# Gate building shared with GpSimd: every fourth group's one-hot rows made token by token, VectorE's keys and gates read from PSUM

## The chip, the cores and the metric

The kernel runs on one core of a Trainium2 chip, in one launch, in float32 (a few index steps in bfloat16 and integers). The metric is device time in microseconds, the median of several runs; one further execution was taken with the hardware profiler.

## The reference

A trunk of two layers over 512 tokens of width 1024. Each layer is a mixer (a Conformer convolution in layer 0, stick-breaking attention in layer 1) and a PEER layer of single-neuron experts; each part is pre-normalised and modulated by adaLN vectors. The change is in the PEER layers:

```
q = (h @ w_q)                                  # 8 heads, 2 halves of 128
s = einsum(q, sub_keys)                        # 128 scores per head and half
top_s, top_i = top_k(s, 16)                    # per half
best_s, best_c = top_k(all sums of the two halves, 16)
experts = i1 * 128 + i2                        # 128 picks a token
gates = softmax(best_s)
act = gelu(u_tab[experts] . h) * gates
y = sum over picks of act * v_tab[experts]
```

## The kernel before, in words

The two tables of a layer have 16384 rows of 1024 floats each. The tokens are split in two halves of 256. The first half is computed densely: TensorE multiplies all 128 blocks of 128 experts (`u_block`, L922, 512 KB of `u_t` each; `v_block`, L931, 512 KB of `pk_v` each), and VectorE multiplies the gelu of a block by a matrix of gates that is zero for experts not picked (L1663). The second half is computed by gathering: for each of 128 picks, in two quarters of 128 tokens, GpSimd asks for one row of either table per token by an indirect DMA (`u_row`, L492; `v_row`, L498; 512 KB each), VectorE makes the dot product (`u_dot`, L1584) and adds the weighted row (`v_add`, L1601). Rows of u land in eight slots, rows of v in four; a request waits until its slot has been used, and requests of u and v alternate on GpSimd's one queue.

The gate matrix is made by TensorE: for each token, a [picks x 128] one-hot of the second key times a [picks x 64] one-hot of the first key weighed by the gate. "First gates" is the stage in which this is done for keys 0 to 63 of the first key, ahead of the dense blocks of round g=0; those for keys 64 to 127 are made between the dense blocks of g=0 (`hots`, `gates_group`). Round g=1 has dense blocks and gathering alone.

First gates has 32 groups of 8 tokens. `picks_t_full` says that keys and gates are turned (picks on partitions) in PSUM (L885), ScalarE copies them to SBUF as `pick_t` (L1244, L1245), and then for each group:

- VectorE, `first_hots`: the first key's one-hots (L1630, 8 tokens x 64), the second key's (L1632, 8 x 128), and gates times the first four tokens' one-hots (L1636). Both buffers (`hot1`, `hot2`) have two slots, so group n may start when TensorE is done with group n-2.
- ScalarE, `weigh_hots`: gates times the other four tokens' one-hots (four operations, L1267).
- TensorE, `first_gates`: 8 matmuls (16 in the profile, two for each) into one of two pairs of PSUM banks (L903). For the even group both banks are called mid, for the odd group they are acc and out_e.
- ScalarE, `take_gates`: two copies of 128x256 to the gate matrix (L1252), which free the pair of banks.

VectorE runs the groups in 8 chunks of four, and behind each chunk one `u_dot` of the first batch of gathered rows (behind the first chunk the softmax of the second half as well, L1577 to L1579). Order on each engine is program order. Ahead of first gates VectorE ranks the last heads (`rank`), GpSimd looks up what they picked (`look_up`, L531 to L543), and VectorE's marking for the next look-up (`choose`, L1491) waits for the look-up two heads back or one. GpSimd's look-up of the last head ends inside first gates; after it come the first eight u rows, then `both`. TensorE clears the banks of the dense sums with 1-row matmuls (`clear`, L889: out_e 0 to 2 before `u_block(0, 0)`, out_e 3 after first gates), and the first `u_block` runs ahead of first gates.

## Time and profile before

| what | value |
|---|---|
| median of 3 runs | 3123.57 us (3122.34 to 3128.29) |
| the profiled execution, own time | 3127.49 us |
| its span, first to last instruction | 3125.7 us |
| TensorE matmul / weight load busy | 2901.2 us (93%) / 2087.0 us (67%) |
| VectorE busy | 2306.6 us (74%) |
| ScalarE busy | 534.6 us (17%) |
| GpSimd busy | 1509.3 us (48%) |
| DMA, mean over the span | 306 GB/s |

The order of time lists an operation's start, its duration, engine, line and tiles; records of one line that follow one another stand in one row with their count, and brackets hold the idle time of the engine before it and what ended that. The stretches view gives, for a window, the busy time and count of records by engine, then the granted TensorE clock as a share of full speed, the busy share of the DMA engines and what they moved. Groups by form give total busy time and the mean duration in ns, then the idle time before. GpSimd is POOL, VectorE DVE, ScalarE ACT, TensorE PE. Positions in us count from the span's start.

### The profile page before, as it was taken

Reading aid. Unit: us, or ns where it says so; the run is one execution under the profiler, and the core shown is the slowest. Engines: PE = TensorE matmul, PEld = TensorE weight load, DVE = VectorE, ACT = ScalarE, POOL = GpSimd, SP = SyncE. Lnnn points to the kernel's source line nnn. Section 1 sums busy time; section 2 is a strip of 40 time slices with the busy share of each in tenths; the row PEclk is TensorE's granted clock in tenths of the full one; section 3 lists DMA queues with packets and bytes.
Section 4 is the critical chain, followed back from the end, with each engine's and each line's share of the span. In section 5 each row is a group of like instructions: output and inputs, shape, how many; then the busy total and the mean of one; then the engine's idle time right before and its main releaser. Section 6 shows DMA issues by size and latency. Waiting matters only on the chain. (4 is left out here: it accounts for less than half of the span.)

```text
span 3125.7 us, 45269 instructions
## 1 busy us (share of the span) xinstructions
PE 2901.2 (93%) x12846; PEld 2087.0 (67%) x12846; DVE 2306.6 (74%) x4886; ACT 534.6 (17%) x1358; POOL 1509.3 (48%) x1567
## 2 busy tenths in 40 slices
PE   6998988999999999999899988969999999999997
PEld 4786777777777665555587866767776676655554
DVE  3999799888878766676522654998788888667666
ACT  2122216100000000000232243152000000000001
POOL 0001354455655676676300252454555555777774
PEclk8998989999999999999999999989999999999999
DMA  7644454799999999999733322336999999999998
GB/s 300 241 175 162 162 210 127 291 409 393 409 410 404 409 410 410 410 410 410 267 140 109 134 81 81 108 121 237 410 406 401 403 405 410 410 410 410 410 410 319
DMA packets 242632, 956.16 MB, mean 306 GB/s; under 512 B 26938, under 2 KB 27114, under 8 KB 224875
## 3 DMA queue, kind: packets, MB, share of 16 engines
q0 software_dynamic: 147456, 536.94, 43.6%
q1 hardware_dynamic: 95082, 418.12, 34.7%
q8 instruction: 41, 0.67, 0.1%
q14 instruction: 53, 0.43, 0.0%
HBM read 952.85 MB, written 2.10 MB: 306 GB/s over the span
## 5 line engine op out<-in xcount | busy, mean ns | idle before, releaser
L931 PE MATMUL out_e<-weights,mod_rows 128*128 128x512 f32 x2048 | 933.4, 599 | 61.6 <-DVE mod_rows L1663 58.6
L922 PE MATMUL acc<-h_t,weights 128*128 128x256 f32 x4096 | 930.7, 380 | 0.0
L922 PEld LDWEIGHTS acc<-h_t,weights 128*128 128x128 f32 x4096 | 781.0, 191 | 218.3 <-issue 121.5
L498 POOL DMA_INDIRECT v_rows<-in_pk_v,idx_now x512 | 634.7, 1240 | 563.7 <-DVE mod_rows L1601 440.1
L1601 DVE SCALAR_TENSOR_TENSOR mod_rows<-v_rows,dots_acts,mod_rows 128x1024 f32<-128x1024 f32 x512 | 657.8, 1285 | 221.8 <-DMA v_rows<-in_pk_v,idx_now 207.7
L931 PEld LDWEIGHTS out_e<-weights,mod_rows 128*128 128x128 f32 x2048 | 376.0, 190 | 471.2 <-issue 371.3
L492 POOL DMA_INDIRECT u_rows<-in_pk_u,idx_now x512 | 576.4, 1126 | 235.7 <-issue 152.1
L1584 DVE SCALAR_TENSOR_TENSOR u_rows<-u_rows,h_rows 128x1024 f32<-128x1024 f32 x512 | 625.8, 1222 | 82.5 <-DMA u_rows<-in_pk_u,idx_now 78.5
L531 POOL CAST top_f<-top_i 128x64 f32<-128x64 uint32 x32 | 7.6, 236 | 717.0 <-DVEq L1542 709.0
L1287 ACT ACTIVATE mod_rows<-acc 128x256 f32<-128x256 f32 x256 | 96.9, 383 | 1168.2 <-PE acc L922 816.9
L612 PE MATMUL acc<-h_t,weights 128*128 128x256 f32 x1024 | 237.4, 393 | 12.5 <-ACT h_t L1085 8.4
L612 PE MATMUL acc<-u_rows,weights 128*128 128x256 f32 x1024 | 228.7, 383 | 5.9 <-ACT u_rows L1085 5.0
L612 PEld LDWEIGHTS acc<-h_t,weights 128*128 128x128 f32 x1024 | 200.7, 198 | 45.7 <-ACT h_t L1085 9.2
L1663 DVE TENSOR_TENSOR mod_rows<-mod_rows,region 128x256 f32<-128x256 f32 x256 | 109.7, 429 | 161.7 <-ACT mod_rows L1287 108.1
L612 PEld LDWEIGHTS acc<-u_rows,weights 128*128 128x128 f32 x1024 | 195.1, 192 | 33.8 <-ACT u_rows L1085 5.6
L1425 DVE SCALAR_TENSOR_TENSOR region<-region,cols 128x256 f32<-128x256 f32 x480 | 191.1, 478 | 0.1
L912 PEld LDWEIGHTS mid<-scratch 128*128 128x128 f32 x1024 | 124.2, 192 | 4.4 <-DVE scratch L1622 1.2
L912 PE MATMUL mid<-scratch 128*128 128x64 f32 x1024 | 121.4, 272 | 0.4 <-DVE scratch L1622 0.4
L604 PE MATMUL acc<-weights,region 128*128 128x256 f32 x512 | 116.9, 386 | 0.5 <-ACT region L1154 0.5
L604 PEld LDWEIGHTS acc<-weights,region 128*128 128x128 f32 x512 | 96.9, 192 | 18.9 <-issue 5.3
L903 PE MATMUL mid<-scratch 128*128 128x128 f32 x512 | 67.3, 286 | 41.0 <-DVE scratch L1636 41.0
L1240 ACT ACTIVATE dots_acts<-dots_acts (+1 forms) x64 | 13.4, 209 | 523.6 <-DVEq L1589 443.3
(246 smaller groups left out, 2362.9 us busy)
## 6 DMA issues: line engine op xcount, KB each, us to landing
weights<-in_u_t SPq DMA_DIRECT2D x256, 512.0 KB
weights<-in_pk_v SPq DMA_DIRECT2D x256, 512.0 KB
weights<-in_pk SPq DMA_DIRECT2D x32, 1024.0 KB, 4.8
v_rows<-in_ada SPq DMA_DIRECT2D x30, 1024.0 KB, 7.2
weights<-in_w_qkv SPq DMA_DIRECT2D x24, 1024.0 KB, 4.8
weights<-in_w_in SPq DMA_DIRECT2D x16, 1024.0 KB, 7.8
weights<-in_ada SPq DMA_DIRECT2D x8, 1024.0 KB, 4.8
weights<-in_w_out SPq DMA_DIRECT2D x8, 1024.0 KB, 4.8
```

The source lines that it names most:

```text
L492: nc.gpsimd.indirect_dma_start(u_rows[:, r, :], None, a["pk_u"], bass.IndirectOffsetOnAxis(ap=idx_now[:, 0, par, r:r + 1], axis=0)).then_i ...
L498: nc.gpsimd.indirect_dma_start(v_rows[:, r % VR, :], None, a["pk_v"], bass.IndirectOffsetOnAxis(ap=idx_now[:, 1, par, r:r + 1], axis=0)).t ...
L604: last = nc.tensor.matmul(to[:, tt * NC:(tt + 1) * NC], lhs(k, tt), w[:, k * NC:(k + 1) * NC], start=k == 0 and bias is None, stop=k == KB ...
L612: last = nc.tensor.matmul(to[:, c * HALF:(c + 1) * HALF], w[:, k * NC + c * P:k * NC + (c + 1) * P], columns_of[h][:, k, :], start=k == 0, ...
L912: last = nc.tensor.matmul(mid[s][:, t * ROUND:(t + 1) * ROUND], hot2[:, s, t, :], hot1[:, s, t, :], start=True, stop=True)
L922: last = nc.tensor.matmul(acc[s][:, 0:HALF], weights[:, s, k * P:(k + 1) * P], h_t[:, k, :], start=k == 0, stop=k == KB - 1)
L931: last = nc.tensor.matmul(out_e[2 * tt + c][:, :], e_act[:, s, tt * P:(tt + 1) * P], weights[:, s, D + c * 512:D + (c + 1) * 512], start=F ...
L1287: nc.scalar.activation(e_act[:, n % 2, :], acc[n % 2][:, 0:HALF], ACT.Gelu).then_inc(e_gelu_ready, 1)
L1425: steps.behind(stt_op(out=to, in0=seen, scalar=tap, in1=to, op0=ALU.mult, op1=ALU.add))
L1584: stt_op(out=u_rows[:, r, :], in0=u_rows[:, r, :], scalar=1.0, in1=h_rows[:, q % 2, :], op0=ALU.mult, op1=ALU.mult, accum_out=dots[:, bass ...
L1601: stt_op(out=y[:, :], in0=v_rows[:, r % VR, :], scalar=acts[:, bass.ds(b * BATCH + r, 1)], in1=y[:, :], op0=ALU.mult, op1=ALU.add).then_in ...
L1663: tt_op(e_now, e_now, gate, ALU.mult).then_inc(e_act_ready, 1)
```

## The change

The groups keep their order on TensorE, but every fourth (n = 3, 7, ..., 31, eight a layer) is made by GpSimd in buffers of its own, one slot each (`pool_hot1` in `region`, `pool_hot2` in `mod_rows`): for each of the 8 tokens one `tensor_scalar` of 128 elements with one per-partition scalar and one of 64 elements with two (`fourth_hots`, 16 operations a group; it weighs all eight tokens, so ScalarE has nothing to weigh there). VectorE makes the other 24 groups, three in each chunk, numbered m on their own; its slots alternate in m. VectorE reads keys and gates in PSUM, where TensorE now turns them (out_e 0 and 1), in place of `pick_t`; ScalarE still copies `pick_t`, for GpSimd, for its own scales and for g=0. Because out_e 0 and 1 hold the keys, they are cleared after first gates. GpSimd asks for the first two u rows of the first batch between the last look-ups, for the other six and the first half of the next batch between its groups. The loops over groups on TensorE, ScalarE and VectorE are written out, and so are the first two batches of `both`.

```diff
--- before.py
+++ after.py
@@ -139,11 +139,11 @@
...
     @contextmanager
-    def loop(self, times, per):
+    def loop(self, times, per, start=0):
...
         base, static = self.count, self.static
-        with self.engine.Fori(0, times) as i:
-            self.count = i * per + base
+        with self.engine.Fori(start, start + times) as i:
+            self.count = i * per + (base - start * per)
             yield i
...
@@ -227,6 +227,9 @@
...
+        pool_hot2 = mod_rows[:, 2 * D:3 * D].rearrange("p (t n) -> p t n", t=GROUP)
+        pool_hot1 = region[:, 0:GROUP * ROUND].rearrange("p (t n) -> p t n", t=GROUP)
+
...
@@ -280,6 +283,7 @@
...
         first_turned = [out_e[2:4], acc]
+        turned_picks = [out_e[0][:, 0:HALF], out_e[0][:, HALF:2 * HALF], out_e[1][:, 0:HALF]]
         mean, var = out_e[1][:, 0:HALF], out_e[2][:, 0:HALF]
...
@@ -356,6 +361,21 @@
...
         block = ctx.enter_context(nc.Block())
+
+        FOURTH = 4
+        ITERS = GROUPS // FOURTH
+        OWN = GROUPS - ITERS
+
+        def own_no(n):
+
+            return n // FOURTH * (FOURTH - 1) + n % FOURTH
+
+        def group_of(m):
+
+            return m // (FOURTH - 1) * FOURTH + m % (FOURTH - 1)
+
+        def by_pool(n):
+            return n % FOURTH == FOURTH - 1
...
@@ -504,14 +524,31 @@
...
-            def both(q, b, par, after):
+            def both(q, b, par, after, between={}, behind_u=None):
                 indices(q, b, par, 1)
...
                         u_row(*after, 1 - par, r)
+                    if r == VR and behind_u:
+                        behind_u()
                     v_row(q, b, par, r)
+                    if r in between:
+                        between[r]()
+
+            def fourth_hots(l, j):
+
+                n = j * FOURTH + FOURTH - 1
+                if j:
+                    pool.wait_ge(gates_full, l * ROUNDS * GROUPS + CREDIT + n - FOURTH + 1)
+                else:
+                    pool.wait_ge(picks_t_ready, l + 1)
+                for t in range(GROUP):
+                    key_1, key_2, gate = (pick_t[:, m, n * GROUP + t:n * GROUP + t + 1] for m in range(3))
+                    nc.gpsimd.tensor_scalar(pool_hot2[:, t, :], iota_keys[:, :], key_2, None, ALU.is_equal)
+                    last = nc.gpsimd.tensor_scalar(pool_hot1[:, t, :], iota_keys[:, 0:ROUND], key_1, gate, ALU.is_equal, ALU.mult)
+                last.then_inc(pool_hots_ready, 1)
...
@@ -568,12 +605,23 @@
...
                             look_up(l, h, head)
-
-                    pool.wait_ge(scores_full, PK[l, 1] + 8)
-                    indices(q, 0, 0, 0) if q else stage_indices(q, 0, 0, 0)
-                    for r in range(BATCH):
+                            if h and head == PH - 3:
+                                pool.wait_ge(scores_full, PK[l, 1] + PH)
+                                indices(q, 0, 0, 0) if q else stage_indices(q, 0, 0, 0)
+                                u_row(q, 0, 0, 0)
+                            elif h and head == PH - 2:
+                                u_row(q, 0, 0, 1)
+
+                    fourth_hots(l, 0)
+                    for r in (2, 3, 4):
                         u_row(q, 0, 0, r)
-                with steps.loop(BATCHES // 2 - 1, 4) as i:
+                    fourth_hots(l, 1)
+                    for r in (5, 6, 7):
+                        u_row(q, 0, 0, r)
+                    fourth_hots(l, 2)
+                    both(q, 0, 0, (q, 1), {r: lambda r=r: fourth_hots(l, r + 3) for r in range(VR)}, lambda: fourth_hots(l, ITERS - 1))
+                    both(q, 1, 1, (q, 2))
+                with steps.loop(BATCHES // 2 - 1 - (q % 2 == 0), 4, int(q % 2 == 0)) as i:
                     for par in range(2):
...
@@ -881,32 +929,34 @@
...
                         src = pick_key[:, tt, m, :] if m < 2 else pick_gate[:, 0, tt, :]
-                        at = m * HALF + tt * P
-                        last = nc.tensor.transpose(mid[at // 512][:, at % 512:at % 512 + P], src, ident[:, :])
+                        last = nc.tensor.transpose(turned_picks[m][:, tt * P:(tt + 1) * P], src, ident[:, :])
                 last.then_inc(picks_t_full, 1)
...
-                for c in range(3):
-                    clear(c)
-                pe.wait_ge(picks_t_ready, l + 1)
-
-                def first_gates(i, s):
-
-                    n = i * 2 + (l * ROUNDS * GROUPS + s)
-                    pe.wait_ge(hots_ready, n + 1)
-                    pe.wait_ge(hots_weighed, i * 2 + (l * GROUPS + s + 1))
-                    pe.wait_ge(gates_ready, n + 1)
+                clear(2)
+
+                def first_gates(n):
+
+                    m = own_no(n)
+                    if by_pool(n):
+                        pe.wait_ge(pool_hots_ready, l * ITERS + n // FOURTH + 1)
+                        ones, twos = pool_hot1, pool_hot2
+                    else:
+                        pe.wait_ge(hots_ready, l * (OWN + GROUPS) + m + 1)
+                        pe.wait_ge(hots_weighed, l * OWN + m + 1)
+                        ones, twos = hot1[:, m % 2], hot2[:, m % 2]
+                    pe.wait_ge(gates_ready, l * ROUNDS * GROUPS + n + 1)
                     for t in range(GROUP):
                         first = t if t < GROUP // 2 else t - 1
-                        last = nc.tensor.matmul(first_banks[s][t // 4][:, t % 4 * NK:(t % 4 + 1) * NK], hot2[:, s, t, :],
-                                                hot1[:, s, first:first + 2, :].rearrange("p t n -> p (t n)"), start=True, stop=True)
+                        last = nc.tensor.matmul(first_banks[n % 2][t // 4][:, t % 4 * NK:(t % 4 + 1) * NK], twos[:, t, :],
+                                                ones[:, first:first + 2, :].rearrange("p t n -> p (t n)"), start=True, stop=True)
                     last.then_inc(gates_full, 1)
...
                     n = i * 2 + (l * ROUNDS * GROUPS + s)
-                    pe.wait_ge(hots_ready, n + 1)
+                    pe.wait_ge(hots_ready, i * 2 + (l * ROUNDS * GROUPS + s + 1 - (l + 1) * ITERS))
                     pe.wait_ge(gates_ready, n + 1)
...
@@ -933,9 +983,11 @@
...
                 u_block(0, 0)
-                with pe.Fori(0, GROUPS // 2) as i:
-                    for s in range(2):
-                        first_gates(i, s)
+                for n in range(GROUPS):
+                    first_gates(n)
+                pe.wait_ge(picks_t_ready, l + 1)
+                for c in range(2):
+                    clear(c)
                 pe.wait_ge(gates_ready, (l * ROUNDS + 1) * GROUPS + CREDIT)
...
@@ -1241,8 +1293,8 @@
...
                 act.wait_ge(picks_t_full, l + 1)
-                nc.scalar.activation(pick_t[:, 0:2, :].rearrange("p m t -> p (m t)"), mid[0][:, :], ACT.Copy)
-                nc.scalar.activation(pick_t[:, 2, :], mid[1][:, 0:HALF], ACT.Copy).then_inc(picks_t_ready, 1)
+                nc.scalar.activation(pick_t[:, 2, :], turned_picks[2], ACT.Copy)
+                nc.scalar.activation(pick_t[:, 0:2, :].rearrange("p m t -> p (m t)"), out_e[0][:, :], ACT.Copy).then_inc(picks_t_ready, 1)
                 exps(l, 1)
...
@@ -1250,7 +1302,7 @@
...
                             last = nc.scalar.activation(
-                                gates_0[:, :, bass.ds(i * (2 * GROUP) + s * GROUP + c * (GROUP // 2), GROUP // 2)],
+                                gates_0[:, :, (2 * i + s) * GROUP + c * (GROUP // 2):(2 * i + s) * GROUP + (c + 1) * (GROUP // 2)],
                                 bank[:, :].rearrange("p (t i) -> p i t", i=NK)[:, c * ROUND:(c + 1) * ROUND, :], ACT.Copy)
...
@@ -1260,23 +1312,22 @@
...
-                def weigh_hots(i, s):
-
-                    act.wait_ge(hots_marked, i * 2 + (l * GROUPS + s + 1))
+                def weigh_hots(m):
+
+                    act.wait_ge(hots_marked, l * OWN + m + 1)
                     for t in range(GROUP // 2, GROUP):
-                        last = nc.scalar.activation(hot1[:, s, t, :], hot1[:, s, t, :], ACT.Copy,
-                                                    scale=pick_t[:, 2, bass.ds(i * (2 * GROUP) + (s * GROUP + t), 1)])
+                        token = group_of(m) * GROUP + t
+                        last = nc.scalar.activation(hot1[:, m % 2, t, :], hot1[:, m % 2, t, :], ACT.Copy,
+                                                    scale=pick_t[:, 2, token:token + 1])
                     last.then_inc(hots_weighed, 1)
...
                 act.wait_ge(picks_t_ready, l + 1)
-                for s in range(2):
-                    weigh_hots(0, s)
-                with act.Fori(0, GROUPS // 2 - 1) as i:
-                    for s in range(2):
-                        take_gates(0, i, s)
-                        weigh_hots(i + 1, s)
-                for s in range(2):
-                    take_gates(0, GROUPS // 2 - 1, s)
+                for m in range(2):
+                    weigh_hots(m)
+                for n in range(GROUPS):
+                    take_gates(0, n // 2, n % 2)
+                    if not by_pool(n) and own_no(n) + 2 < OWN:
+                        weigh_hots(own_no(n) + 2)
                 row_gelu(2 * l, 0)
...
@@ -1622,28 +1673,27 @@
...
-                def first_hots(i, s):
-                    dve.wait_ge(gates_full, i * 2 + (l * ROUNDS * GROUPS + s + 1))
-                    tokens = bass.ds(i * (2 * GROUP) + s * GROUP, GROUP)
-                    own = bass.ds(i * (2 * GROUP) + s * GROUP, GROUP // 2)
+                def first_hots(m):
+                    n, s = group_of(m), m % 2
+                    dve.wait_ge(gates_full, l * ROUNDS * GROUPS + (n + 1 if m < 2 else group_of(m - 2) + 1 + CREDIT))
+                    tokens = slice(n * GROUP, (n + 1) * GROUP)
+                    own = slice(n * GROUP, n * GROUP + GROUP // 2)
                     wide, full, half = [P, GROUP, ROUND], [P, GROUP, NK], [P, GROUP // 2, ROUND]
                     tt_op(hot1[:, s, :, :], iota_keys[:, 0:ROUND].unsqueeze(1).to_broadcast(wide),
-                          pick_t[:, 0, tokens].unsqueeze(2).to_broadcast(wide), ALU.is_equal).then_inc(hots_marked, 1)
+                          turned_picks[0][:, tokens].unsqueeze(2).to_broadcast(wide), ALU.is_equal).then_inc(hots_marked, 1)
                     tt_op(hot2[:, s, :, :], iota_keys[:, :].unsqueeze(1).to_broadcast(full),
-                          pick_t[:, 1, tokens].unsqueeze(2).to_broadcast(full), ALU.is_equal)
-                    dve.wait_ge(hots_marked, i * 2 + (l * GROUPS + s + 1))
+                          turned_picks[1][:, tokens].unsqueeze(2).to_broadcast(full), ALU.is_equal)
+                    dve.wait_ge(hots_marked, l * OWN + m + 1)
                     mine = hot1[:, s, 0:GROUP // 2, :]
-                    tt_op(mine, mine, pick_t[:, 2, own].unsqueeze(2).to_broadcast(half), ALU.mult).then_inc(hots_ready, 1)
+                    tt_op(mine, mine, turned_picks[2][:, own].unsqueeze(2).to_broadcast(half), ALU.mult).then_inc(hots_ready, 1)
...
                 dve.wait_ge(h_rows_ready, 2 * l + 2)
-                pairs = GROUPS // 2 // BATCH
-                for r in range(BATCH):
-                    with dve.Fori(r * pairs, (r + 1) * pairs) as i:
-                        for s in range(2):
-                            first_hots(i, s)
-                    if r == 0:
+                for j in range(ITERS):
+                    for m in range(j * (FOURTH - 1), (j + 1) * (FOURTH - 1)):
+                        first_hots(m)
+                    if j == 0:
                         softmax(l, 1)
-                    u_dot(2 * l, 0, r)
+                    u_dot(2 * l, 0, j)
                 dots_done(2 * l, 0)
...
```

## Rows read from the trace of the kernel before

**Rows 1.** the stretches view, layer 0 (us; busy us and count by engine, TensorE clock, DMA share, GB/s).

```profile
540.00:560.00 20.00, 17.10 (x130) 15.18 (x130) 18.11 (x27) 13.82 (x47) 0.00 (x0) 1.00 0.00 0
...
650.00:700.00 50.00, 50.00 (x203) 34.62 (x202) 39.47 (x55) 4.68 (x11) 25.86 (x27) 1.00 1.02 408
...
1200.00:1250.00 50.00, 45.53 (x155) 28.69 (x155) 34.89 (x49) 2.93 (x9) 33.95 (x30) 1.00 1.03 409
```

**Rows 2.** the order of time in one chunk, layer 0 (start us, us, idle before and releaser).

```profile
503.45 1.16 PE L903 MATMUL acc<-scratch 128*128 128x128 f32 x8
...
503.59 0.69 DVE L1630 TENSOR_TENSOR scratch<-iota_keys,mod_rows 128x512 f32<-128x512 f32 x1 [0.20 <-PE mid L903]
504.20 1.22 DVE L1632 TENSOR_TENSOR scratch<-iota_keys,mod_rows 128x1024 f32<-128x1024 f32 x1
...
505.34 0.42 DVE L1636 TENSOR_TENSOR scratch<-scratch,mod_rows 128x256 f32<-128x256 f32 x1
...
505.81 2.05 PE L903 MATMUL mid<-scratch 128*128 128x128 f32 x16 [0.31 <-DVE scratch L1636]
...
507.75 1.22 DVE L1584 SCALAR_TENSOR_TENSOR u_rows<-u_rows,h_rows 128x1024 f32<-128x1024 f32 x1
...
508.89 0.69 DVE L1630 TENSOR_TENSOR scratch<-iota_keys,mod_rows 128x512 f32<-128x512 f32 x1
```

**Rows 3.** the order of time, layer 0, from the banks' clearing to the second chunk.

```profile
468.73 5.48 PE L889 MATMUL out_e<-keep_past 1*128 1x512 f32 x6
474.14 6.53 PE L922 MATMUL acc<-h_t,weights 128*128 128x256 f32 x16
...
475.11 2.17 DVE L1632 TENSOR_TENSOR scratch<-iota_keys,mod_rows 128x1024 f32<-128x1024 f32 x1
...
480.33 0.30 POOL L543 TENSOR_TENSOR pick_idx<-pre_idx,best_of 128x32 f32<-128x32 f32 x1
...
486.77 0.28 DVE L1577 TENSOR_REDUCE gate_sum<-pick_gate 128x8 f32<-128x128 f32 x1
...
488.29 1.22 DVE L1584 SCALAR_TENSOR_TENSOR u_rows<-u_rows,h_rows 128x1024 f32<-128x1024 f32 x1
...
491.64 2.05 PE L903 MATMUL mid<-scratch 128*128 128x128 f32 x16 [2.68 <-DVE scratch L1636]
```

**Rows 4.** the order of time, layer 0, end of the first gates.

```profile
557.51 1.06 PE L903 MATMUL out_e<-scratch 128*128 128x128 f32 x8
...
559.31 1.12 PE L889 MATMUL out_e<-keep_past 1*128 1x512 f32 x2 [0.75 <-ACT region L1252]
...
560.36 3.72 PE L922 MATMUL acc<-h_t,weights 128*128 128x256 f32 x16
```

**Rows 5.** the order of time, layer 1, the same stage.

```profile
2033.92 0.69 DVE L1491 TENSOR_TENSOR u_rows<-place_i,dots_acts 128x1024 bf16<-128x1024 uint16 x1 [0.56 <-POOL pick_idx L543]
...
2045.13 0.93 DVE L1630 TENSOR_TENSOR scratch<-iota_keys,mod_rows 128x512 f32<-128x512 f32 x1
...
2049.16 3.76 PE L903 MATMUL mid<-scratch 128*128 128x128 f32 x16 [15.08 <-DVE scratch L1636]
...
2062.30 2.53 PE L903 MATMUL mid<-scratch 128*128 128x128 f32 x16 [2.72 <-DVE scratch L1636]
...
2130.54 1.06 PE L903 MATMUL out_e<-scratch 128*128 128x128 f32 x8
```

**Rows 6.** GpSimd's operations and one of VectorE's from PSUM, groups by form.

```profile
L557 POOL TENSOR_SCALAR_AFFINE_SELECT u_rows<-u_rows 128x128 f32<-128x128 f32 x32 | 25.8, 843 | 0.4 <-ACT u_rows L1175 0.4
...
L471 POOL TENSOR_SCALAR_AFFINE_SELECT ident<-ident 128x128 f32<-128x128 f32 x1 | 0.3, 289 | 0.2 <-POOL ident L470 0.2
...
L1404 DVE TENSOR_TENSOR scratch<-acc,mod_rows 128x512 f32<-128x512 f32 x16 | 11.0, 689 | 64.2 <-PE acc L604 63.6 <-DVE region L1425 0.2
```

**Rows 7.** the order of time, GpSimd's row requests, layer 0.

```profile
509.78 1.74 POOL L492 DMA_INDIRECT u_rows<-in_pk_u,idx_now  x1 [5.91 <-DVE u_rows L1584]
...
571.55 0.94 POOL L492 DMA_INDIRECT u_rows<-in_pk_u,idx_now  x1 [0.30 <-issue]
```

1 line of the change is left out of this document (added).

## The prediction

> **What bounds the kernel now.** I read the stretches view first, then the order of time in the stage that changes, then the groups by form for prices.
>
> The stretches view tells three regimes apart [rows 1]. In first gates (540 to 560) VectorE is busy 18.1 of 20 us, TensorE 17.1 at full clock, GpSimd and DMA nothing at all: every slot for rows and blocks is full and nothing can be asked for until the stage ends. In round g=0 TensorE is busy 50.00 of 50 us, so it is the bound (DMA at 408 GB/s is close behind). In round g=1 TensorE falls to 45.5 of 50 and DMA stays at 409 GB/s: the transfers bound it. Both later regimes begin from full slots and take a fixed time, so what first gates gets shorter moves all that follows. That holds for both layers, since each PEER layer is followed by work that needs its output.
>
> In first gates the order of time shows who sets the pace [rows 2]. A group costs VectorE 0.61 + 1.14 + 0.33 us by the starts of its three operations (503.59 to 505.67, 2.08 us), TensorE 2.06 us. A slot comes free when TensorE ends a group (503.45, the start of the next), VectorE starts 0.14 later (503.59), and TensorE starts on that slot at 505.81, 2.36 us after it freed it. With a dot (507.75 to the next group's start at 508.89, 1.14 us), four groups cost VectorE 4 x 2.08 + 1.14 = 9.5 us, TensorE 8.2. From the second chunk's first group (491.64) to the end of the last (557.51 + 1.06 = 558.57) seven chunks take 66.9 us, 9.6 each [rows 3, 4]. VectorE is the bound, TensorE is 1.4 us a chunk behind it.
>
> **The change, part by part.**
>
> *Three groups of four on VectorE.* Call a chunk A, B, C, P, with P made by GpSimd. VectorE: 3 x 2.08 + 1.14 = 7.4 us. TensorE: 4 x 2.06 = 8.24. So the bound becomes TensorE, plus what the two slots still cost. Let TensorE end A at 0. It ends B at 2.06; C needs A's slot, so starts at 2.36 and ends at 4.42; P ends at 6.48. VectorE meanwhile is done with C's one-hots at 2.22, with the dot at 3.36, with the next A at 5.44, in time for 6.48, so next A ends at 8.54. It makes next B by 7.5 and then waits for A's end. One stall of 0.30 us a chunk: 8.54 us. ScalarE is busy 13.8 of 20 us now, 6.6 a chunk [rows 1], and a fourth of its weighing goes: it stays hidden.
>
> *Seven chunks* from the second A on: its end, then the rest, is 8.54 x 7 = 59.8 us against 66.9: 7.1 us less. In layer 1 the same stretch (2062.30 to 2131.60) takes 69.3, of which some is a half-clock spell: the group at 2062.30 takes 2.53 us for its records and the next pair too is late, after 2.72 us of idling [rows 5]. With P behind C that idle time shrinks to about 0.6, so I count 59.8 there too: 9.5 less.
>
> *The first chunk.* Now it begins with a collision: the look-up of the last head runs on GpSimd while VectorE makes groups 0 and 1, and one-hots that take 1.22 us take 2.17 [rows 2, 3]. Also TensorE clears three banks at half clock (5.48 us for 6 records, 1.83 a bank) ahead of the 6.53 us of `u_block` and is first free at 480.7 [rows 3]. With two clears moved, `u_block` ends at 468.73 + 1.83 + 6.53 = 477.1; group 0 ends at 479.2, C's one-hots run 479.3 to 481.4, softmax 1.52 (486.77 to 488.29), dot 1.14, and A's one-hots are ready 2.2 later: 486.3 in place of 491.64, 5.2 us less [rows 3]. In layer 1 VectorE's first group starts at 2045.13, its one-hots would be ready by 2047.7 in place of 2049.16, and groups 0 and 1 keep their half clock (3.76 us for the first). The same addition comes to 2058.4 against 2062.30: 3.9 less, with 0.4 us taken off for the next item [rows 5].
>
> *First rows between look-ups.* Each index cast and request stands in GpSimd's queue ahead of a look-up for which VectorE's `choose` waits; that wait already ends last once in layer 1 (0.56 us, at 2033.92) [rows 5]. A cast with its wait and a request of 0.94 + 0.30 us [rows 7] is some 2.3 us, put into a gap that is about that wide, so I take 0 in layer 0 and 0.4 in layer 1, bounds 0 to 2.3. The rows themselves bring nothing: the first dot comes when VectorE gets to it (488.29), not when the row lands. They only free GpSimd for its own group 0.
>
> *Keys and gates from PSUM.* The nearest row is the 128x512 product with one input in PSUM, 689 ns, against 0.69 us for L1630 [rows 2, 6]. I take 0.1 us a chunk on the path of C (0.8 a layer), bounds 0 and 2. What it does for the collision is more: VectorE then has one SBUF input in each one-hot operation and two only in the dot. The Trainium skill ("SBUF — State Buffer", Who interferes with whom) has the rule for this: a VectorE instruction with two SBUF inputs excludes a GpSimd instruction that reads SBUF for its whole length, one with a single SBUF input does not. The collision row above agrees; that the single-input form is free no row here shows, and by the rule the sum stays as it is.
>
> *Clears behind first gates.* Out_e 0 and 1 are now cleared after the last group, about 1.05 us each at full clock (559.31 to 560.36), and ScalarE's last copies hide only 0.75 of it: `u_block` starts 1.4 us later than it would [rows 4]. TensorE is the bound from there, so -1.4 a layer (bounds 0 and 2.1).
>
> *GpSimd's groups.* P has one slot, so GpSimd can start when TensorE ends P and must be done 6.48 us later, when the next P is due. It also issues a u and a v request a chunk, 2 x (0.94 + 0.30) = 2.5 us, about what P takes on TensorE, and loses up to 1.1 us to the dot. So per chunk: 2.5 + 1.1 + 16x, x being the mean of one `tensor_scalar`. This hides under 8.54 while x is below 0.30 us. No row shows the form (a per-partition scalar). From below: a 128-element select with VectorE quiet takes 0.289 [rows 6], half of mine have 64 elements, so 0.2 is the low end. From above: the same select beside VectorE's two-input operations takes 0.843 [rows 6]. I take 0.27, nearest to the quiet row, since VectorE is quiet in this sense but for the dot: 7.9 us, hidden.
>
> **Sum.** Layer 0: 7.1 + 5.2 - 0.8 - 1.4 = 10.1. Layer 1: 9.5 + 3.9 - 0.8 - 1.4 = 11.2. Together 21.3 us off the profiled execution's own 3127.49 (span 3125.7): 3106.2. The median of the runs is 3.9 below that execution, so on it: 3102.
>
> **Rivals.**
>
> 1. *GpSimd sets the pace, slower.* With x above 0.30 the chain over the one slot of P rules. The last look-up ends at 480.6 today [rows 3], some 2 us of that by the collision, so a layer then ends first gates at about 478.5 + 16x + 7 x (3.6 + 16x) + 4.5 (two more sets of requests, the last P) in layer 0's positions. Less 1.4 for the clears, that equals today's 558.6 at x = 0.38. At x = 0.5 it is 572: 13.7 + 1.4 later, for both layers some +28, time 3152. At 0.84, if VectorE's single-input operations excluded it after all, some 40 us a layer more again: above 3220. For it: two scalars read through pointers, 16 instructions where VectorE needs three. Against: the quiet select at 0.289 for 128 elements.
> The Trainium skill ("GPSIMD Engine Reference", Performance pitfalls for Q7 kernels) speaks against the change here: each small read command costs about 102 cycles that don't overlap the one before. Three scalars a token by that figure would be an estimated 2 us a group more, x = 0.27 + 0.13 = 0.40, and a time near 3128. No row here shows it.
> 2. *GpSimd sets the pace, gain shrinks.* x between 0.30 and 0.38: each 0.01 costs 1.3 us a layer, so 3102 to 3123, say 3112.
> 3. *The gain is lost behind the stage.* If DMA rather than TensorE bounded g=0, the later clears and the earlier rows would change nothing, and a gain of only the DMA-idle time would remain; as no DMA runs in most of the stage [rows 1], even so most of it stays. The clears' delay and the look-ups' could be at their bounds (2.1, 2.3): 3110.
> 4. *It doesn't do what it says*: VectorE's operations from PSUM slower by 0.3 us each, 0.9 on C's path each chunk, 14 in all: 3115. The row at 689 ns speaks against.
>
> **How the numbers follow.** The forecast has 0.50; rival 1 0.20 (its lower half, to 3152, has most of that), rival 2 0.17, rivals 3 and 4 0.13 together. 0.2%, some 6 us, is about what a measurement of this kernel can tell from no change. Faster (below 3117): 0.50 + 0.13 + two thirds of rival 2 = 0.74. Same (3117 to 3130): the rest of rival 2 and a little of rival 1, 0.10. Slower: 0.16. Range: TensorE's hard limit of 8.24 a chunk with nothing lost to PSUM or clears would give 8 us more, 3094; upward it takes in rivals 2 to 4 and the edge of 1, 3126. The likeliest case by itself: 3096 to 3108.
>
> **What would show it.** TensorE's groups (L903) in fours without idle time but 0.3 us in front of C, first gates 12 to 13 us shorter in each layer, the second A near 486.3; VectorE idle about 1 us a chunk, waiting for TensorE; GpSimd's `tensor_scalar` at 0.2 to 0.3 us, and TensorE never released by it; one-hots at 1.22 us from the first group on; `u_block` about 3.2 us after the last group's end. It is wrong if TensorE waits for GpSimd before P (x too small here), if VectorE's one-hots beside GpSimd's are stretched (the single-input form collides), or if the g=0 stretch is no longer at 50.00 of 50 (the gain given back).

## The result and the profile after

| | before | after |
|---|---|---|
| median of the runs (us) | 3123.57 (3122.34 to 3128.29, 5 runs) | 3187.44 (3184.93 to 3191.72, 5 runs) |
| span of the profiled execution (us) | 3125.7 | 3185.7 |
| GpSimd busy in it (us) | 1509.3 (48%) | 1631.1 (51%) |

The ratio is 1.0201, 95% interval [1.0189, 1.0213]: slower, by 64 us, where the prediction had 3102 and a range of 3094 to 3126. The two profiled executions lie 60.0 us apart.

The stretches view of the same three windows as in [rows 1]:

```profile
core 0: us, PE busy (x) PEld busy (x) DVE busy (x) ACT busy (x) POOL busy (x), PEclk, DMA share, GB/s
540.00:560.00 20.00, 11.35 (x78) 10.78 (x77) 11.50 (x17) 8.36 (x30) 17.98 (x28) 0.88 0.17 53
650.00:700.00 50.00, 50.00 (x208) 35.51 (x207) 38.52 (x54) 4.46 (x11) 26.76 (x30) 1.00 1.03 410
1200.00:1250.00 50.00, 45.43 (x157) 28.94 (x156) 34.79 (x49) 2.88 (x9) 34.98 (x30) 1.00 1.03 410
```

The two later regimes are as they were; the loss lies in first gates, where VectorE fell from 18.1 of 20 us to 11.5, TensorE from 17.1 to 11.4, and GpSimd went from nothing to 18. One chunk of layer 0 in order of time, against [rows 2]:

```profile
531.17 2.08 PE L953 MATMUL acc<-region,mod_rows 128*128 128x128 f32 x8 [4.09 <-POOL region L550]
531.27 1.03 POOL L512 DMA_INDIRECT u_rows<-in_pk_u,idx_now  x1 [0.15 <-issue]
532.61 0.94 POOL L518 DMA_INDIRECT v_rows<-in_pk_v,idx_now  x1 [0.30 <-issue]
533.04 1.81 PE L953 MATMUL out_e<-region,mod_rows 128*128 128x128 f32 x8
534.95 0.61 POOL L549 TENSOR_SCALAR mod_rows<-iota_keys,mod_rows 128x128 f32<-128x128 f32 x1 [1.41 <-PE out_e L953]
536.67 0.69 DVE L1682 TENSOR_TENSOR scratch<-iota_keys,out_e 128x512 f32<-128x512 f32 x1 [6.44 <-PE mid L953]
...
538.74 1.22 DVE L1635 SCALAR_TENSOR_TENSOR u_rows<-u_rows,h_rows 128x1024 f32<-128x1024 f32 x1
538.98 1.43 POOL L550 TENSOR_SCALAR region<-iota_keys,mod_rows 128x64 f32<-128x64 f32 x1
...
545.03 2.08 PE L953 MATMUL acc<-region,mod_rows 128*128 128x128 f32 x8 [4.10 <-POOL region L550]
```

The rows show a loop of two partners. GpSimd works from 534.95 to about 545.0 on its group. Then TensorE, which had waited 4.1 us for it, takes the group in 3.7 us (531.17 to 534.85) at a granted clock of 0.54 of full speed: 2.08 us for eight matmuls, where the same eight take 1.16 in [rows 2]. Only then may GpSimd begin again. That is 10.1 + 3.8 = 13.9 us a chunk, where [rows 2] have 9.6. The requests (531.27 to 533.55) lie hidden beside TensorE's part. VectorE, freed as intended, waits 6.4 us a chunk. The 1.43 us at 538.98 are GpSimd's instruction beside the dot, the one operation of VectorE's in this stage with two inputs in SBUF; beside the one-hots its instructions keep to some 0.6. The prices by form:

```profile
L550 POOL TENSOR_SCALAR region<-iota_keys,mod_rows 128x64 f32<-128x64 f32 x128 | 87.9, 687 | 0.0
L549 POOL TENSOR_SCALAR mod_rows<-iota_keys,mod_rows 128x128 f32<-128x128 f32 x128 | 76.2, 595 | 13.7 <-PE out_e L953 13.1
L1684 DVE TENSOR_TENSOR scratch<-iota_keys,out_e 128x1024 f32<-128x1024 f32 x48 | 58.1, 1211 | 0.0
```

The start and the end of the stage in layer 0, against [rows 3, 4]:

```profile
479.32 0.69 DVE L1682 TENSOR_TENSOR scratch<-iota_keys,out_e 128x512 f32<-128x512 f32 x1 [0.91 <-PE mid L953]
484.13 0.68 DVE L1682 TENSOR_TENSOR scratch<-iota_keys,out_e 128x512 f32<-128x512 f32 x1
489.27 2.07 PE L953 MATMUL acc<-region,mod_rows 128*128 128x128 f32 x8 [5.70 <-POOL region L550]
...
586.17 2.08 PE L953 MATMUL acc<-region,mod_rows 128*128 128x128 f32 x8 [4.10 <-POOL region L550]
589.59 2.85 PE L936 MATMUL out_e<-keep_past 1*128 1x512 f32 x6
592.37 5.41 PE L972 MATMUL acc<-h_t,weights 128*128 128x256 f32 x16
599.34 3.22 PE L981 MATMUL out_e<-weights,mod_rows 128*128 128x512 f32 x7
```

The stage ends at 589.6 in place of 558.6, and the first block of the second table product starts 33.2 us later (599.34 against 566.14). Layer 1 adds 27.8 (its first such block starts at 2200.20 against 2139.16). These 61 us are the whole difference of the two profiled executions.

### The profile page after: what moved, and what is told of

Read it like the earlier page. It is cut to its first block, busy times and chain, and to the rows that moved or that the text cites. A ratio compares the mean times of both kernels' runs of the same rounds, so it can differ in the third digit from the quotient of the medians.

```text
span 3185.7 us, 44262 instructions
## 1 busy us (share of the span) xinstructions
PE 2916.0 (92%) x12846; PEld 2109.9 (66%) x12846; DVE 2263.8 (71%) x4838; ACT 517.9 (16%) x1294; POOL 1631.1 (51%) x1823
## 4 chain that ended last, share of the span: by engine, by line
PE 48%; DMA 14%; issue 11%; POOL 11%; DVE 6%; ACT 2%; POOLq 0%; DVEq 0%; ACTq 0%
PE acc L972 14%; PE out_e L981 14%; DMA v_rows<-in_pk_v,idx_now 14%; PE acc L660 8%; PE acc L652 4%; PE mid L962 3%; POOL region L550 3%; POOL v_rows L518 2%; POOL mod_rows L549 2%; POOL u_rows L512 2%; DVE mod_rows L1652 2%; PE acc L953 1%; PE out_e L953 1%; PE mid L771 1%; POOL idx_now L507 1%
## 5 line engine op out<-in xcount | busy, mean ns | idle before, releaser
L518 POOL DMA_INDIRECT v_rows<-in_pk_v,idx_now x512 | 623.5, 1218 | 533.4 <-DVE mod_rows L1652 411.2
L512 POOL DMA_INDIRECT u_rows<-in_pk_u,idx_now x512 | 565.6, 1105 | 200.7 <-issue 145.0
L1682 DVE TENSOR_TENSOR scratch<-iota_keys,out_e 128x512 f32<-128x512 f32 x48 | 32.7, 681 | 91.9 <-PE mid L953 91.9
L953 PE MATMUL acc<-region,mod_rows 128*128 128x128 f32 x128 | 32.6, 435 | 68.7 <-POOL region L550 68.7
```

The lines of the kernel that those rows point to most:

```text
L512: nc.gpsimd.indirect_dma_start(u_rows[:, r, :], None, a["pk_u"], bass.IndirectOffsetOnAxis(ap=idx_now[:, 0, par, r:r + 1], axis=0)).then_i ...
L518: nc.gpsimd.indirect_dma_start(v_rows[:, r % VR, :], None, a["pk_v"], bass.IndirectOffsetOnAxis(ap=idx_now[:, 1, par, r:r + 1], axis=0)).t ...
```

## The experiments

Each result is the ratio to the kernel before on the same chip. The chips differ by up to 9 us, so ratios are compared, not medians. "Under" and "over" are that ratio times 3123.6.

**1. All groups back on VectorE, all else as changed.**

```
-            return n % FOURTH == FOURTH - 1
+            return False            # by_pool; own_no(n) = n, group_of(m) = m
```

> GpSimd makes no one-hots of the first gates; VectorE makes all 32 groups of a layer, as before the change, with a dot after every fourth. All other parts of the change stay: keys and gates read from PSUM, the stage unrolled, first rows requested between look-ups, two clears behind the stage. Theory A (GpSimd's token-by-token groups are the whole loss: 16 instructions of 0.58 us on one slot): a chunk goes back to VectorE's 9.5 to 9.6 us, the first chunk keeps what it won (5.2 and 3.9 us), the clears cost 1.4 a layer: 3123.6 - 3.8 - 2.5, so 3117, between 3113 and 3121. Theory B (a good part of the loss lies in the clears, the early rows or the reads from PSUM): 3140 to 3187. Theory C (those parts bring nothing either way): 3123 to 3127.

0.9987 [0.9978, 0.9995], 4 us under (3119.5, within A's 3113 to 3121). The loss is all in GpSimd's groups. The steady chunk is 9.56 us. The second A starts on TensorE at 487.43 where the kernel before has 491.64 [rows 3]: 4.2 us of the 5.2 expected. Some of this was given back at once in layer 0:

```profile
487.43 2.05 PE L954 MATMUL mid<-scratch 128*128 128x128 f32 x16 [2.67 <-issue]
489.89 0.69 DVE L1683 TENSOR_TENSOR scratch<-iota_keys,out_e 128x512 f32<-128x512 f32 x1 [2.52 <-PE mid L954]
```

The first of these idle times is no loss: it is TensorE's wait for VectorE over softmax and dot, 2.68 us in [rows 3] too, under another name. The second is a stop. VectorE ended its one-hots at 487.37, its next slot had been free since 484.76, and yet it and ScalarE (idle 2.88 us) start only at 489.89, both at the same moment. Layer 1 has no such stop of more than 1 us.

**2. Every eighth group by GpSimd token by token.**

```
-        FOURTH = 4
+        FOURTH = 8
```

> GpSimd makes every eighth group token by token instead of every fourth; VectorE makes 28 of 32, its eight dots spread evenly between them. All else as in the changed kernel. Theory A (a GpSimd group costs some 10 us including what the dot blocks, on one slot; it harms only because 10.1 + 3.6 is more than the chunk has): eight groups now take VectorE 7 x 2.08 + 2 x 1.14 = 16.8 us and TensorE 16.5, GpSimd needs about 12.5 with its requests and is hidden; TensorE stays at full clock. 8.4 us for four groups where before has 9.6: 8.3 us less over the seven later chunks, 5.2 (3.9) for the first, 1.4 back for the clears: 12.1 and some 12 in layer 1, so 3099, between 3094 and 3106. Theory B (GpSimd's work beside VectorE's slows VectorE or TensorE, whatever its share): half of the loss stays, above 3150. Theory C (the gain is taken back later): within 3118 to 3127.

0.9973 [0.9961, 0.9985], 8.4 us under; 24 were expected by A (3099). TensorE never waits for GpSimd here, as A said: half the share fits. The rest went two ways. VectorE and TensorE stop together once in each layer (TensorE for 2.56 us before 519.41 and 4.93 before 2091.66, VectorE for 2.69 and 4.70). And there is the end of the stage:

```profile
551.29 3.23 PE L933 MATMUL out_e<-keep_past 1*128 1x512 f32 x6
554.45 6.67 PE L969 MATMUL acc<-h_t,weights 128*128 128x256 f32 x16
```

Three clears in a row, and then the next product mostly at half clock: 6.67 us against 3.72 in [rows 4]. In layer 1, in layer 0 of experiment 1 and in the changed kernel it is 5.41. The clears alone don't decide it, since in experiment 6, layer 0, the same three are followed by a product at full clock (in layer 1 it takes 5.12):

```profile
549.69 3.72 PE L973 MATMUL acc<-h_t,weights 128*128 128x256 f32 x16
```

**3. VectorE reads keys and gates from SBUF.**

```
-                          turned_picks[0][:, tokens]...
+                          pick_t[:, 0, tokens]...        # also [1] and [2]
```

> The changed kernel, but VectorE's one-hots read keys and gates from the copy in SBUF, as before the change, so that each of its three operations has two SBUF inputs. Theory A (such an operation and GpSimd's exclude one another, a single-input one and GpSimd's do not): the 7.4 us of VectorE and the 9.4 of GpSimd in a chunk no longer overlap, 16.8 us a chunk or a little more in place of 13.8: 3 us x 7 x 2 more, some 3230, GpSimd's instructions 1.2 us or more in the mean where they meet VectorE's. Theory B (the source of VectorE's inputs doesn't matter here): 3187, GpSimd's instructions at 0.6 us.

1.0453 [1.0438, 1.0468], 141 us over, some 79 us slower than the changed kernel. A had the direction, but only 43 of these 79. GpSimd's 64-element form keeps its median (582 ns), has a mean of 961 and a maximum of 3227: some wait for whole operations of VectorE's. The chunk, from one group of GpSimd's to the next:

```profile
531.55 2.07 PE L953 MATMUL acc<-region,mod_rows 128*128 128x128 f32 x8 [7.80 <-POOL region L550]
550.13 2.08 PE L953 MATMUL acc<-region,mod_rows 128*128 128x128 f32 x8 [8.33 <-POOL region L550]
```

18.6 us in place of 13.9, where A had 16.8. So the runs agree with the rule cited in the prediction (the Trainium skill, "SBUF — State Buffer", Who interferes with whom): beside VectorE's operations with two SBUF inputs GpSimd's 0.58 us become 1.1 to 3.2 (the row at 539.64 has 3.23), beside those with one they stay at 0.57 to 0.59 in the changed kernel. The read from PSUM was worth its place.

**4. and 5. What GpSimd's instruction costs, by form.** Both are the changed kernel with other instructions for a group's tokens:

```
+  t < 2: as they are      t < 4: constants in place of pointers
+  t < 6: one pointer, 16, 112 and 64 elements      else: tensor_tensor subtract
```

> The changed kernel with GpSimd's instructions for the eight tokens of a group in four forms, two tokens each, on lines of their own: (1) as they are, one pointer at 128 elements and two at 64; (2) the same with constants in place of the pointers; (3) one pointer at 16, at 112 and at 64 elements; (4) a tensor_tensor subtract with the key broadcast, 128 and 64 elements. So the one-hots of six tokens in eight are not what they should be. Theory P (the pointer's read is the price): form 2 falls to 0.2 to 0.3 us, form 3 stays at 0.57 at every size. Theory I (the instruction is): every form is 0.55 to 0.6 at every size. Theory E (elements are): 16 elements take under 0.2, 112 take 0.5, form 2 at 128 takes 0.55. The time of the whole lies between 3150 and 3187 by P and near 3187 by I and E.

```
+  wide subtract and wide is_equal of 1024 elements for the second keys
+  first keys, 64 elements: subtract with a pointer; mult, add with constants;
+                           is_equal with a constant; mult, add with two pointers
```

> The changed kernel with other forms in GpSimd's groups: the second keys by one wide tensor_tensor subtract and one wide tensor_scalar is_equal over 1024 elements, and, for the first keys, tensor_scalar over 64 elements in four forms, two tokens each: subtract with one pointer, mult and add with constants, is_equal with a constant, mult and add with two pointers. The gates of these groups are not what they should be. Theory A (every tensor_scalar has the fixed price): all four forms at 0.55 to 0.57 us, the wide is_equal under 3 us. Theory C (the comparison is the slow operation): mult and add at 0.22 to 0.3 us with constants or pointers, is_equal at 0.56, and the wide is_equal at some 3 us or more.

None of the theories as a whole. Each is one profiled execution, from which only prices of instructions are read. One line each: minimum, median and maximum in ns. First the run of experiment 4, then that of 5:

```profile
L550 POOL TENSOR_SCALAR mod_rows<-iota_keys,mod_rows x32: 593/606/634, 475.0 to 2148.6; 128x128 f32<-128x128 f32 x32
L551 POOL TENSOR_SCALAR region<-iota_keys,mod_rows x32: 566/568/587, 475.6 to 2149.2; 128x64 f32<-128x64 f32 x32
L553 POOL TENSOR_SCALAR mod_rows<-iota_keys x32: 519/520/1581, 477.3 to 2150.6; 128x128 f32<-128x128 f32 x32
L554 POOL TENSOR_SCALAR region<-iota_keys x32: 422/422/1438, 477.8 to 2151.1; 128x64 f32<-128x64 f32 x32
L556 POOL TENSOR_SCALAR mod_rows<-iota_keys,mod_rows x32: 310/315/1291, 480.1 to 2153.7; 128x16 f32<-128x16 f32 x32
L557 POOL TENSOR_SCALAR mod_rows<-iota_keys,mod_rows x32: 550/552/1567, 480.4 to 2154.0; 128x112 f32<-128x112 f32 x32
L558 POOL TENSOR_SCALAR region<-iota_keys,mod_rows x32: 430/434/1484, 481.0 to 2154.5; 128x64 f32<-128x64 f32 x32
L560 POOL TENSOR_TENSOR mod_rows<-iota_keys,mod_rows x32: 388/392/397, 482.6 to 2155.6; 128x128 f32<-128x128 f32 x32
L561 POOL TENSOR_TENSOR region<-iota_keys,mod_rows x32: 282/285/290, 483.0 to 2155.9; 128x64 f32<-128x64 f32 x32
```

```profile
L558 POOL TENSOR_SCALAR region<-iota_keys,mod_rows x32: 427/440/1329, 483.6 to 2137.6; 128x64 f32<-128x64 f32 x32
L560 POOL TENSOR_SCALAR region<-iota_keys x32: 232/233/240, 484.6 to 2138.2; 128x64 f32<-128x64 f32 x32
L562 POOL TENSOR_SCALAR region<-iota_keys x32: 356/362/373, 485.0 to 2138.7; 128x64 f32<-128x64 f32 x32
L564 POOL TENSOR_SCALAR region<-iota_keys,mod_rows x32: 377/378/390, 485.7 to 2139.4; 128x64 f32<-128x64 f32 x32
```

In the second fence L558 is subtract with a pointer, L560 mult and add with constants, L562 is_equal with a constant, L564 mult and add with two pointers. For is_equal the price is a sum. Elements: (552 - 315) / 96 = 2.5 ns each for is_equal. What is left at none: 315 - 16 x 2.5 = 275 ns, with one pointer. Each pointer: 434 - 362 = 72 ns, (568 - 422) / 2 = 73 and (378 - 233) / 2 = 73. So about 200 fixed, 2.5 an element, 73 a pointer, and 60 for a second operation (422 - 362). For 64 elements, two pointers and two operations: 200 + 160 + 146 + 60 = 566, measured 568; that is partly by construction, but 128 elements with one pointer (593, measured 606) and the wide one of 1024 elements (2760, measured 2787) were not used for it. Mult and add don't follow it: 233 with constants, less than is_equal's 362, although there are two operations. Nor is it the comparison that is dear, as theory C had it, since subtract with one pointer takes 440 and is_equal with one 434. Only mult and add were cheaper here. And a tensor_tensor subtract with the key broadcast takes 392 and 285 ns, less than any tensor_scalar here that reads a pointer at that size. That the two forms of the changed kernel cost the same is a coincidence: the smaller one has a pointer and an operation more.

**6. A group shared: GpSimd makes half of it.**

```
-                    nc.gpsimd.tensor_scalar(pool_hot2[:, t, :], iota_keys[:, :], key_2, None, ALU.is_equal)
+  VectorE, behind its second own group of a chunk:
+                    tt_op(pool_hot2[:, :, :], iota_keys..., turned_picks[1]..., ALU.is_equal).then_inc(shared_ready, 1)
```

> Every fourth group is shared: GpSimd makes the weighed one-hots of the first key token by token (8 instructions in place of 16), VectorE makes those of the second key in one wide operation of 1.21 us, put behind its second own group of a chunk. All else as in the changed kernel. Theory A (each of GpSimd's instructions costs some 0.57 us, whatever it reads): a group of GpSimd's falls to 8 x 0.57 + 0.9 for the dot = 5.5 us, which with its requests hides in the chunk; VectorE has 3 x 2.05 + 1.21 + 1.14 = 8.5, TensorE 8.24; a chunk takes 8.6 in place of 13.8, TensorE keeps its full clock. Against before: 7 x 1.0 and 5.2 (3.9) less, 2 to 4 lost behind the stage and up to 2.7 by an issue stall, some 6 to 9 us a layer: 12 to 18 us faster than before. Theory B (what hurts is that GpSimd works beside VectorE at all): half of the loss stays, slower than before by 25 us.

0.9929 [0.9915, 0.9942], 22 us under, more than A's 12 to 18. GpSimd's eight instructions (mean 666 ns with what the dot blocks) nearly hide: TensorE waits for them 7 times, 5.8 us in all over both layers. The granted clock is 1.00 and VectorE is the bound, with 8.46 us from dot to dot in most chunks:

```profile
490.00:540.00 50.00, 44.15 (x373) 42.26 (x373) 49.54 (x72) 32.38 (x118) 44.17 (x63) 1.00 0.43 138
L550 POOL TENSOR_SCALAR region<-iota_keys,mod_rows 128x64 f32<-128x64 f32 x128 | 83.7, 666 | 4.6 <-PE out_e L954 3.9
```

**7. The same work in twice the instructions.** As 6, each of GpSimd's instructions cut in two of 32 elements.

```
+                    for k in (slice(0, ROUND // 2), slice(ROUND // 2, ROUND)):
```

> The shared version with each of GpSimd's instructions cut into two of 32 elements: 16 in place of 8 for a group, the same elements read and written, the same two pointers each. Nothing else changes. Theory A (the price is a fixed one for each instruction: 418 ns at 16 elements, 552 at 64 in the forms run, so some 0.46 at 32): a group takes 16 x 0.46 + 0.9 = 8.3 us in place of 5.4, TensorE's part of the loop 2.06 at full clock: 10.4 to 10.8 us a chunk in place of 8.75, the stage some 14 us longer in each layer, 20 to 32 us slower than the shared version, and slower than the kernel before. Theory B (the price goes by elements): the same time as the shared version, 0.7% under the kernel before.

1.0063 [1.0044, 1.0082], 20 us over: 42 more than 6 for the same elements, where A had 20 to 32 more and B none. By the sum above a half costs 200 + 80 + 146 + 60 = 486 ns, measured 462 at the median. A left TensorE at full clock, which is part of what it missed:

```profile
502.70 8.25 POOL L551 TENSOR_SCALAR region<-iota_keys,mod_rows 128x32 f32<-128x32 f32 x16
511.01 2.08 PE L955 MATMUL acc<-region,mod_rows 128*128 128x128 f32 x8 [3.81 <-POOL region L551]
```

GpSimd's group of 8.3 us makes TensorE wait 3.8, and it comes back at half clock (granted 0.50), 2.08 in place of 1.16. In the next chunk it waits 1.27 and takes 1.16.

**8. No clears.** The first block of the second table product starts the sums, in three kernels:

```
+                        v_block(i * 2 + n, 0, start=first and n == 0)
-                clear(2), clear(0), clear(1), clear(3)
```

Shared, as 6:

> As the shared version, but the four output banks are not cleared at all: the first block of the second table product starts the sums itself (start=True; its loop's first pass is written out). Theory A (the two clears behind first gates cost their own length and let TensorE's clock fall, so that the next product of 16 instructions takes 5.4 to 6.7 us in place of 3.7): 2 to 3.8 us less a layer than with the clears, 4 to 7.6 in all. Theory B (the clears lie beside ScalarE's table load and gelu, 2.6 us, and cost nothing): the same time as the shared version.

Every eighth group, as 2:

> Every eighth group by GpSimd token by token, as in the run before, and no clears. Theory A (behind the stage 3.8 us a layer went to the clears and to the half clock that followed): 7 us less than with clears, so 15 to 16 us faster than before. Theory B (the gain went elsewhere): 8 us faster than before, as with the clears.

All groups on VectorE, as 1:

> VectorE makes all groups, the stage unrolled, no clears. Theory A (an unrolled stage stalls for issue by 2.7 us or more while rows are requested): the stall of 2.67 us on TensorE is there in both layers, and the time is that of the all-VectorE run less 2 to 4 us for the clears: 6 to 8 us under before. Theory B (the stalls come from where the code happens to lie; the every-eighth version lost its own with the clears): no stall above 1 us, 9 to 12 us under before, or more than the loops' 3 us.

0.9925 [0.9912, 0.9939], 0.9943 [0.9930, 0.9957] and 0.9969 [0.9959, 0.9980]: 23, 18 and 10 us under. Against the same kernels with clears the second and the third gain 9 and 6 us, and the first 1 us, which can't be told from nothing, as its theory B had it. The second's total is near A's, the third's is B's. For the second, the end of the stage is now

```profile
547.01 1.06 PE L946 MATMUL out_e<-region,mod_rows 128*128 128x128 f32 x8
548.86 3.69 PE L965 MATMUL acc<-h_t,weights 128*128 128x256 f32 x16 [0.80 <-issue]
```

with full clock behind it (3.69 for 6.67). From the last group's end to the first block of the second product it is 7.6 us in both layers, where experiment 2 has 11.3 and 9.7: 5.8 us. Its stops are gone too, though it is unrolled as before. So A's total came in part from elsewhere: it had put all its gain down to the clears. The all-VectorE one has a stop of 1.00 us on VectorE in layer 0 and none in layer 1. So unrolling alone doesn't bring the stops, and experiment 10 has them without it.

**9. and 10. In loops, with early rows and with late rows.** The kernel before, with PSUM reads, no clears and, in 9, early rows; no one-hots by GpSimd, no groups written out. The second takes out

```
-                            if h and head == PH - 3: ... u_row(q, 0, 0, 0)
-                            elif h and head == PH - 2: u_row(q, 0, 0, 1)
```

> The kernel before with VectorE making all groups in its loops, plus: keys and gates read from PSUM, first rows requested between look-ups, and no clears at all. No one-hots by GpSimd, nothing unrolled. Theory A (the unrolled stage costs an issue stall of some 2.7 to 4.9 us a layer, on several engines at once, while rows are being requested; a loop doesn't): no stall above 1 us on TensorE and VectorE in either layer; first chunk 5.2 and 3.9 less, 1 us from the steady chunks, nothing lost behind the stage: 10 to 13 us faster than before. Theory B (the stall comes with the early rows and not with the unrolling): the stall stays, 5 to 8 us faster.

> The version with loops and no clears, its first rows requested behind the last look-up, as before the change. Theory A (the early requests bring nothing, since the first dot comes later than its row in either case, and cost a look-up's wait of 0.3 to 0.6 us in layer 1): the same time as with early rows, or up to 2 us less: 3 to 5 us under before. Theory B (they bring something): 2 us or more slower than with them.

0.9989 [0.9980, 0.9998] and 1.0022 [1.0012, 1.0031]: 3 us under and 7 over. For 9 both theories failed: no stop, as A said, but not its gain. For 10 theory B held: late rows cost 10 us more. With late rows (first) TensorE idles for 7.5 us in layer 0 and 6.3 in layer 1, 2.7 of each being its usual wait for softmax and dot; with early ones (second) it has that wait alone:

```profile
484.00:488.00 4.00, 0.17 (x2) 0.00 (x0) 0.73 (x2) 0.00 (x0) 3.21 (x3) 1.00 0.96 351
488.00:492.00 4.00, 0.30 (x1) 0.30 (x2) 2.50 (x4) 2.26 (x8) 2.30 (x5) 0.53 1.00 388
```

```profile
484.00:488.00 4.00, 1.33 (x12) 1.14 (x12) 3.96 (x8) 1.60 (x6) 3.17 (x4) 1.00 0.98 358
488.00:492.00 4.00, 3.76 (x32) 3.38 (x30) 3.81 (x7) 2.88 (x11) 2.08 (x3) 1.00 0.85 291
```

VectorE's row shows the stop of layer 0 by itself (in layer 1 it is 3.49 us):

```profile
489.50 0.69 DVE L1628 TENSOR_TENSOR scratch<-iota_keys,out_e 128x512 f32<-128x512 f32 x1 [4.77 <-remote]
```

Late rows alone don't make it, since the kernel before asks for them as late and has none. What differs is GpSimd's pace. Beside VectorE's operations with two SBUF inputs a request takes up to 1.93 us, in experiment 10 most take 0.94, so that eight requests span 13.5 us (481.87 to 495.38) there and 10.3 (477.76 to 488.01) here:

```profile
483.33 1.93 POOL L492 DMA_INDIRECT u_rows<-in_pk_u,idx_now  x1 [0.30 <-issue]
482.94 0.94 POOL L493 DMA_INDIRECT u_rows<-in_pk_u,idx_now  x1 [0.30 <-issue]
```

A dense burst alone isn't enough either: experiment 9 has 358 GB/s at 484 to 488 and no stop. The cause is open.

The loops of 9 gained 3 us where the unrolled stage of 8 gained 10. 2.6 us of that are in the steady chunks: 9.67 us in layer 0 and 9.82 in layer 1, against 9.56 in both, seven times. The rest I didn't settle.

## Why the prediction was wrong

- *GpSimd's groups: the failed step.* The term x, the mean of one of its instructions, was 0.27 us. The means are 0.595 (128 elements) and 0.687 (64 elements, with the dot's blocking in it; its median is 0.577), so x without the blocking is 0.58, and the 16 take 9.3 us in place of 4.3. With that GpSimd's part was not hidden, as the sum had it, but set the pace of every chunk. The step went by the quiet select in [rows 6], 289 ns for 128 elements. The form runs show what it left out: is_equal (520 ns at 128 elements with a constant) and the pointers, 73 ns each, 24 of them in a group, 1.75 us. The upper bound, 0.84, held it. The trace of the kernel before also had a tensor_scalar of GpSimd's, which the prediction doesn't use: L542, mult and add with constants, 32 elements, median 227 ns. It would have shown a quarter of the elements at nearly the price assumed.
- *Rival 1 is what happened.* It had 0.20. By its own steps, 0.58 is 0.08 above the 0.5 for which it gave 3152, and each 0.01 costs 1.28 us a layer: 3172. The other 15 us are 1.0 a chunk (13.9 against 3.6 + 9.3). Its sum had 3.6 beside 16x, for requests and dot. In fact the requests lie beside TensorE's part, which takes 3.8 at a clock near half, and the dot blocks 0.9. At full clock TensorE's part would be about 2.1 us and the requests' 2.3 would end last, an estimate from these rows that puts a chunk at 12.4 us; so the clock is enough to account for the 15 us. Experiments 1, 2, 6 and 7 show the mechanism from four sides: away with it, half as often, half of each, and that half in twice the instructions.
- *One slot, or too much work?* No run separates them. GpSimd's group and its requests take 10.0 + 2.3 us, so even with a second slot a chunk would be some 12.4 us by an estimate from these rows, more than the 9.6 of before. What GpSimd's wait for TensorE costs, through the single slot and the half clock together, is then 1.5 us of the 13.9; the price of the instructions is the rest.
- *The pointers.* The runs have 73 ns for each, which should have been a term of the sum. The page cited against the change pointed the right way (the Trainium skill, "GPSIMD Engine Reference", Performance pitfalls for Q7 kernels, some 102 cycles for each small read command). At the 1.2 GHz that this page gives for GpSimd (Specifications) that is an estimated 85 ns. That a pointer is such a read the page doesn't say, and no run here shows more than that the two figures are near. The pointers alone make x 0.38, so most of the miss is elsewhere.
- *Seven chunks at 8.54.* Not tested: no run has VectorE at three groups of four and GpSimd hidden. Experiment 6 comes near in number, (545.04 - 484.61) / 7 = 8.63, but there VectorE is the bound, with its extra 1.21 us, and not TensorE. That its 22 us under before are what the prediction had for the whole change is luck.
- *The first chunk.* Right: the second A's one-hots were forecast for 486.3 and end where the next group's begin, at 486.2 (484.13 + 2.06). In layer 1 it is 13.0 us from VectorE's first one-hots to this point (2074.86 to 2087.84) against 17.2 (2045.13 to 2062.30), 4.2 less where 4.3 were forecast before the look-ups' 0.4. The collision with the look-up is gone: the one-hots take 1.21 us from the first group on.
- *Keys and gates from PSUM.* 1211 ns for 1024 elements in place of 1.22 us: it costs nothing, the lower bound. What it protects from is experiment 3.
- *Clears.* 1.4 us a layer taken; from the stage's end to the first v block it is 9.7 us (589.6 to 599.34) against 7.6, so 2.1, the upper bound. In layer 0 of experiment 2 it was 3.7, with the product at 6.67 us.
- *First rows between look-ups.* Taken at nothing in layer 0. Experiments 9 and 10, on two chips, put it at 10 us, give or take 4, in a kernel whose GpSimd has no groups, through stops whose cause is open (4.8 and 3.5 us on VectorE). The changed kernel has no such stop, and its DMA share beside GpSimd's groups is mostly low (0.17 in the window at 540).

The version to keep is that of experiment 6 or its form without clears: 0.9929 and 0.9925 of the time before.

## What to carry to other kernels

Before moving work to an engine, find a row of that engine's with the same operation and the same kind of operands, and count its scalars; where there is none, the forecast is no better than the wider bound. Here the nearest row of another operation was off by a factor of two. A helper with a single buffer must fit its whole round trip, the partner's part at half clock included, into the chunk: half of each group (experiment 6) gave what the whole could not.

## What the runs showed of the hardware

- A GpSimd tensor_scalar with is_equal on 128 partitions: about 200 ns, 2.5 ns an element, 73 ns a pointer. Subtract with a pointer costs the same (440 against 434 ns at 64 elements), mult and add less (233 with constants). The wide is_equal of 1024 elements had a median of 2787 ns, the tensor_tensor subtract 1903.
- TensorE came back at half clock after waits of 3.8 and 4.1 us (2.08 us for eight matmuls against 1.16), and after one of 2.56 in experiment 2 (3.68 for sixteen), while after the wait of 2.68 in [rows 3] the sixteen took 2.05. Behind three one-row clears the next product took from 3.72 to 6.67 us.
- VectorE and ScalarE, in experiments 2 and 10 TensorE too, can stop together (VectorE for 1.0 to 4.8 us, in experiments 1, 2, 8 and 10), in stretches in which rows are being requested and the DMA share is 0.9 to 1.0; where it strikes moves with small edits. The Trainium skill ("Runtime: NRT & Kernel Launch", Instruction fetch mechanics) has each engine fetch its instructions by a DMA queue of its own and calls the cost mostly hidden. A fetch held up behind the rows would be one cause, but the traces don't bear it out: the DMA view has one packet of an instruction queue at 517 to 518, where the stop of experiment 2 in layer 0 ends, and none in the other stops (480 to 490 in experiments 1 and 8, 470 to 500 and 2056 to 2068 in experiment 10, 2080 to 2092 in experiment 2). The cause stays open.
